# Gate and up products of the experts: eight matmuls with high weight halves, then eight with low halves, in each bank

## What is computed

```python
aff = jax.nn.softmax(logits, axis=0)
gate, idx = lax.top_k(aff, cap)                 # cap = 2 * n // 16: 128 prompt or 64 sample tokens
xg = hf[idx]
a = jnp.einsum('ecd,edf->ecf', xg, w_gate)      # 1024 -> 2048 for each of 16 experts
b = jnp.einsum('ecd,edf->ecf', xg, w_up)        # 1024 -> 2048
out = jnp.einsum('ecf,efd->ecd', jax.nn.silu(a) * b, w_down) * gate[..., None]
```

## Time and profile before

| | |
|---|---|
| median of 3 runs | 2634.75 us |
| span of the profiled execution | 2632.3 us |
| TensorE busy, share of the span | 2541.6 us, 97% |
| its weight loads (PEld) | 2338.2 us, 89% |
| VectorE busy | 1825.0 us, 69% |
| ScalarE busy | 1398.8 us, 53% |
| HBM traffic, mean | 189 GB/s |
| mean granted TensorE clock | 0.983 of full |

### The profile page before, as it was taken

One profiled execution on the slowest core, in us unless ns is written; L12 is line 12 of the kernel. 1 busy time (PEld: TensorE's weight loads), 2 busy tenths in 40 slices (PEclk: granted clock), 3 DMA queues, 4 the chain that ended last, 5 costly groups with the idle time before them and its releaser, 6 DMA issues.

```text
span 2632.3 us, 39845 instructions
## 1 busy us (share of the span) xinstructions
PE 2541.6 (97%) x15910; PEld 2338.2 (89%) x15910; DVE 1825.0 (69%) x2098; ACT 1398.8 (53%) x1769; POOL 273.7 (10%) x269
## 2 busy tenths in 40 slices
PE   8999799997996999999999999999999999999997
PEld 8889699976885999989999898998989989899996
DVE  7878899965367766767666676666766667676674
ACT  4232667677223555656555565554655556565553
POOL 3735000000000000101001010010101101010000
PEclk9999899998996999999999999999999999999999
DMA  7344000012225777867778677787768768677773
GB/s 245 106 167 161 9 1 1 1 57 90 105 104 193 236 232 235 256 224 253 224 254 250 224 252 226 246 245 241 246 223 256 239 232 261 224 250 227 240 246 108
DMA packets 339356, 499.38 MB, mean 190 GB/s; under 512 B 10224, under 2 KB 287088, under 8 KB 337264
## 3 DMA queue, kind: packets, MB, share of 16 engines
q1 hardware_dynamic: 332144, 471.76, 54.3%
q0 software_dynamic: 7040, 25.17, 3.8%
HBM read 457.05 MB, written 39.85 MB: 189 GB/s over the span
## 4 chain that ended last, share of the span: by engine, by line
PE 91%; DVE 5%; ACT 1%; POOL 1%; issue 1%; DMA 1%; SPq 0%; ACTq 0%; POOLq 0%; DVEq 0%
PE psum L1616 31%; PE psum L1618 14%; PE psum L1345 8%; PE psum L1346 8%; PE psum L1347 8%; PE psum L1482 5%; PE psum L1638 5%; PE psum L1639 5%; PE psum L1457 3%; PE psum L1469 3%; DVE q_st L1011 1%; DVE conv L922 1%; PE psum L1547 1%; PE psum L1601 0%; DVE top L1156 0%
## 5 line engine op out<-in xcount | busy, mean ns | idle before, releaser
L1247 DVE TENSOR_TENSOR w_lo<-raw,w_hi 128x2048 fp32r<-128x2048 f32 x384 | 880.1, 2292 | 495.4 <-ACT w_hi L806 492.8
L1616 PE MATMUL psum<-xgT,w_hi 128*128 128x384 f32 x4096 | 1168.7, 360 | 2.4 <-issue 2.4
L1618 PE MATMUL psum<-xgT,w_lo 128*128 128x192 f32 x4096 | 1026.5, 251 | 0.0
L806 ACT CAST w_hi<-raw 128x2048 fp32r<-128x2048 f32 x384 | 733.4, 1910 | 333.6 <-PE psum L1639 332.8
L1618 PEld LDWEIGHTS psum<-xgT,w_lo 128*128 128x128 f32 x4096 | 783.9, 191 | 0.6
L1616 PEld LDWEIGHTS psum<-xgT,w_hi 128*128 128x128 f32 x4096 | 770.6, 188 | 3.5 <-issue 2.8
L922 DVE SCALAR_TENSOR_TENSOR conv<-conv,colp 128x1024 f32<-128x1024 f32 (+1 forms) x240 | 252.8, 1053 | 5.0
L1345 PE MATMUL psum<-w_hi,hid_st 128*128 128x512 f32 x512 | 212.9, 416 | 0.0
L1346 PE MATMUL psum<-w_lo,hid_st 128*128 128x512 f32 x512 | 202.5, 396 | 0.0
L1347 PE MATMUL psum<-w_hi,hid_st 128*128 128x512 f32 x512 | 202.4, 395 | 0.0
L1638 PE MATMUL psum<-w_hi,hid_st 128*128 128x512 f32 x508 | 201.1, 396 | 0.0
(11 more groups left out here) (212 smaller groups left out, 3344.2 us busy)
## 6 DMA issues: line engine op xcount, KB each, us to landing
raw<-in_w_gate_dram SPq DMA_DIRECT2D x128, 1024.0 KB, 5.3
raw<-in_w_up_dram SPq DMA_DIRECT2D x128, 1024.0 KB, 5.3
raw<-in_w_down_dram SPq DMA_DIRECT2D x128, 1024.0 KB, 4.9
wi_raw<-in_w_in_dram SPq DMA_DIRECT2D x28, 256.0 KB, 5.0
wi_kept<-wi_hi SPq DMA_DIRECT2D x14, 512.0 KB, 6.0
wi_kept<-wi_lo SPq DMA_DIRECT2D x14, 512.0 KB, 6.3
wi_hi<-wi_kept SPq DMA_DIRECT2D x7, 1024.0 KB, 4.8
wi_lo<-wi_kept SPq DMA_DIRECT2D x7, 1024.0 KB, 7.0
```

The lines of the kernel that those rows point to most:

```text
L806: act.copy(w_hi[:, j % SPLIT_SLOTS, :], raw[:, j % RAW_SLOTS, :]).then_inc(e_hi, 1)
L1247: dve.tensor_tensor(w_lo[:, j % SPLIT_SLOTS, :], raw[:, j % RAW_SLOTS, :], w_hi[:, j % SPLIT_SLOTS, :].bitcast(F32), ALU.subtract).then_in ...
L1616: pe.matmul(bank[:, 0:2 * CAP], w_hi[:, slot, w0:w0 + P], xgT[:, half, k, :], start=(k == 0), stop=False, skip_group_check=True)
L1618: last = pe.matmul(bank[:, 0:CAP], w_lo[:, slot, w0:w0 + P], xgT[:, half, k, 0:CAP], start=False, stop=(k == KD - 1), skip_group_check=True)
```

## The change

In each of the two banks of a chunk the loop over k is split in two: first the eight matmuls with high weights, then the eight with low weights. The matmuls, their operands, their flags (the first clears the bank, the last closes it), their weight loads and all waits and signals are the same; only the order within the bank is another.

```diff
                 for i in range(2):
+                    bank = psum[:, 2 * up + i, :]
                     for k in range(KD):
                         w0 = k * CCOLS + i * P
-                        bank = psum[:, 2 * up + i, :]
                         pe.matmul(bank[:, 0:2 * CAP], w_hi[:, slot, w0:w0 + P], xgT[:, half, k, :],
                                   start=(k == 0), stop=False, skip_group_check=True)
+                    for k in range(KD):
+                        w0 = k * CCOLS + i * P
                         last = pe.matmul(bank[:, 0:CAP], w_lo[:, slot, w0:w0 + P], xgT[:, half, k, 0:CAP],
                                          start=False, stop=(k == KD - 1), skip_group_check=True)
                 last.then_inc(e_used, 1)
```

## The result

The changed kernel takes 2644.3 us (median of 6 runs, 2643.51 to 2645.86), the kernel before 2634.93 us beside it (6 runs, 2634.27 to 2638.18). The ratio is 1.0034 with a 95% interval of 1.0024 to 1.0044: slower by 9.4 us, 0.34%, where I had called up to 0.2%, 5 us, "no change". The number lies in the range given, 2625 to 2662, but outside the forecast's own 2630 to 2640, on the side of the lesser chance.

What follows compares the result with a forecast made beforehand. TensorE was taken to bound the kernel. Per bank, 1387.2 ns high plus 890.4 ns low gave 2277.6 against 2276.0 before: +1.6 ns x 512 = +0.8 us, so 2635.6 us; range 2625 to 2662.

Steps and rivals of the forecast that it cites:

- the first rival: High matmuls in a row take the down products' constant, 20.3 for 13.4 ns: 24.7 us more, 2660.3 us; chance 0.20.
- My own sign of being wrong: Wrong if low spacing matched no load-bound row, or if high matmuls' spacing depended on what stands next to them.
- What bounds the kernel: TensorE, busy 97% of the span and 91% of the chain; every ns on a matmul counts about once.
- The split of the pair: High-low pair of 284.5 ns: high bound by its columns, 173.4 ns, low by the next weight load, 111.3 ns.
- that rival: Two loads could be ahead, so runs of low matmuls uncover loads: 64 us slower, 2699 us; chance 0.04.
- Item 1: Per bank, eight high matmuls, each with the next load hidden under it: 8 x 173.4 = 1387.2 ns.
- Item 2: Per bank, eight low matmuls, each bound by the load of the next: 8 x 111.3 = 890.4 ns.
- Item 3: Seven low matmuls add to the same 192 columns one after another: nothing added, as in the router.

Runs made afterwards that it cites:

- groups of four: Changed kernel with four high, four low, four high, four low matmuls in each bank, in place of eights: 2651.13 us, ratio 1.0063.
- the wide kernel: Kernel before, high and low in turn, but the low matmuls take all 384 columns too: 2889.75 us (2 runs).
- the wide eights: Changed kernel's order, eight high then eight low, but the low matmuls take all 384 columns too: 2889.34 us (2 runs).
- The swap: Kernel before with `hid_st` and `xgT`, of equal size, in each other's place in SBUF: 2621.97 us, ratio 0.9948.
- the swap of the same two buffers: Changed kernel (eights) with `hid_st` and `xgT` in each other's place in SBUF: 2623.46 us, ratio 0.9956 to the kernel before.
- the pairs apart: Kernel before with each bank ordered H H L H L H L L H L H L H L H L: 2646.52 us, ratio 1.0041.

## Why the prediction was right, and where it was not

The time, 2644.3 us, is in the range of 2625 to 2662 and 8.7 us over the 2635.6 forecast. I gave "no change" 0.62 and "slower" 0.26; measured was slower by 0.34%, clear of 0.2 by its interval. That the range holds it is in part luck: its upper end was the price of the first rival, which had the size wrong. My own sign of being wrong came true as well, that the high ones' spacing depends on what stands next to them. Point by point:

- **What bounds the kernel.** Right. Every ns of the chunk means came out in the end: 17.8 x 512 = 9.1 us of 9.4; in groups of four 62.3 x 256 = 15.9 us of 16.4.
- **The split of the pair**, 173.4 for the columns and 111.3 for the load. Right, and the best of the working: low matmuls in a row cost 111 to 112 ns, the wide kernel was forecast at 2890 and measured 2889.8. One load is ahead, never two; that rival is out.
- **Item 1, eight high matmuls at 173.4.** This term failed. Five of eight cost 173.3; the first three cost some 15 ns more together. The run takes 1402 ns for the 1387.2 of the sum, and 14.8 x 512 = 7.6 us are most of the 8.7 missed.
- **Item 2, the low ones at 111.3.** Right as a cost. The run takes 891.3 ns for the 890.4 of the sum, 0.5 us in all. I had taken one price for a low matmul in turn and in a run, and they differ by 2.5 ns in eight; the sum had 1.6 of them by chance, from setting a pair of 284.7 made of two rows against the 284.5 measured. Together with 0.2 us from rounding that 284.5, 8.3 of the 8.7 us are found.
- **Item 3, adding to the same columns.** Nothing of it was seen, though no run tests it by itself: the wide eights do the same at 173 ns without a stall.
- **The first rival, the larger constant.** It named the right run and was too large: 6.9 ns on seven of eight would be 24.7 us, and the loss dies out after three. It had the cause wrong, too: in the wide kernels rows of hidden loads alone cost 173.3 ns each. I had written that nothing I saw said why the down products have the larger constant, and left it there. The swap shows that the place of the operands sets it, and the swap of the same two buffers takes away nearly all of the step as well.

I had also a row against me that I hadn't used: in the kernel before, behind the transposes that begin at 787.37, these two starts of 512-column matmuls are six spacings apart, 0.231 us each, before they settle at 0.227:

```profile
788.48 0.39 PE L1346 MATMUL psum<-wo_lo,mT_hi 128*128 128x512 f32 x1
...
789.86 0.39 PE L1346 MATMUL psum<-wo_lo,mT_hi 128*128 128x512 f32 x1
```

It looks like the same thing in another place, a run of load-bound matmuls and a slow start behind it. The last five before it settles, 236, 228, 232, 231 and 227 ns, are those of the down products of the swapped kernel before they settle. No run was made for it.

## What to carry to other kernels

Before grouping or interleaving matmuls, split the measured spacing into columns + constant and load: where one kind is bound by its load and the other by its columns, and only one load is ahead, the sum of the costs is the same in every order; here no grouping won anything, and each step between runs of four to sixteen cost 15 to 22 ns. If the constant of a stream differs between stages of a kernel (here 20 against 13 ns), try changing places of two buffers of equal size; here that was worth 13.4 us, more than the order of the matmuls either way. Compare spacings of starts, never the busy time of a line, when the order of lines changes.

## What the runs showed of the hardware

- The same down products cost 233.6 ns each, or once settled 226.5 in the swapped kernel, by where the stationary operand lies in SBUF. The Trainium skill ("TensorE: Matmul & The Clock Gate", Step-by-step, point 1) says that the load of the next weights has a read port of its own and takes nothing from the running matmul; here loads that are wholly hidden make some 7 ns a matmul more or less by the place they read from (with stationary blocks of `xgT` and no buffer moved it is 227.0, with fixed blocks of `hid_st` 233.2), so the running matmuls weren't free of them. Whether it is read bandwidth that they take, no run shows.
- A stream of matmuls has paces that last: with the pairs apart, the same instructions took 4580.0 ns a chunk in nine experts and 4613.3 in seven, each through the whole expert, and four pairs in turn took 0.2925 us each where the steady kernel takes 0.2845.
- At half clock (granted 0.50) the constant is nil: 426 ns for 512 columns, while a load takes 212 ns for the 111 at full clock.
